# Layer 2 of a mixture-of-experts trunk: experts in fixed order, one at a time, in place of a computed order with six pairs

## What is computed

```python
g_sel = top-1 group of 4;  e_sel = top-2 of the 8 experts in that group      # per token
combine = (T, 32), two entries per token, the others zero
y = 0
for e in range(32):
    he = silu(t @ w_gate[e]) * (t @ w_up[e])          # 1024 -> 256, twice
    y = y + combine[:, e, None] * (he @ w_down[e])    # 256 -> 1024
```

## Time and profile before

| what | value |
|---|---|
| median of 3 runs | 684.5 us |
| the profiled execution's own time | 686.16 us |
| its span in the trace | 684.5 us |
| TensorE busy | 630.1 us, 92% of the span |
| VectorE, ScalarE, GpSimd busy | 36%, 18%, 9% |
| DMA queue of SyncE | 272.65 MB, 95.4% of 16 engines' span |
| mean granted TensorE clock | 0.987 of full speed |

### The profile page before, as it was taken

The page is one execution under the profiler, slowest core; times in us unless marked ns, Lnnn a source line. Parts: engine busy times, 40 slices in busy tenths (PEclk is TensorE's granted clock), DMA queues, the critical chain, the costliest instruction groups (busy, mean ns, idle before and its releaser), DMA issues.

```text
span 684.5 us, 12945 instructions
## 1 busy us (share of the span) xinstructions
PE 630.1 (92%) x4798; PEld 384.4 (56%) x4798; DVE 249.7 (36%) x664; ACT 120.8 (18%) x313; POOL 61.0 (9%) x187
## 2 busy tenths in 40 slices
PE   4899899999899999999999999999999996898995
PEld 1455465555455455556888788877644442455442
DVE  1024423222322223235679497137423230222233
ACT  4013530000000000014144234138000000000003
POOL 7000011101101101100000000001111110000100
PEclk9999999999999999999999999999999998999998
DMA  8999999999999999999997989966999999999992
GB/s 353 417 419 423 426 425 428 430 432 432 425 432 431 432 425 426 426 421 419 420 420 314 374 344 431 421 272 252 373 414 425 426 424 421 426 427 422 429 413 100
DMA packets 27690, 273.32 MB, mean 399 GB/s; under 512 B 3188, under 2 KB 3700, under 8 KB 4984
## 3 DMA queue, kind: packets, MB, share of 16 engines
q1 hardware_dynamic: 27640, 272.65, 95.4%
HBM read 271.59 MB, written 1.05 MB: 398 GB/s over the span
## 4 chain that ended last, share of the span: by engine, by line
PE 84%; DMA 9%; issue 4%; DVE 1%; ACT 1%; SPq 1%; ACTq 0%; DVEq 0%
PE bank L847 74%; DMA ring<-in_ada_w_dram 9%; PE bank L1055 7%; PE bank L1264 2%; PE bank L1582 1%; SPq L509 0%; ACT hx L2097 0%; PE bank L1436 0%; PE bank L1443 0%; DVE ye L2138 0%; ACT reg_b L1903 0%; DVE ye L2135 0%; ACTq L180 0%; DVE xh L2404 0%; DVE reg_c L2138 0%
## 5 line engine op out<-in xcount | busy, mean ns | idle before, releaser
L847 PE MATMUL bank<-ring,xh 128*64 128x256 f32 (+2 forms) x2496 | 305.7, 429 | 29.9 <-issue 29.0
L847 PEld LDWEIGHTS bank<-ring,xh 128*64 128x64 f32 (+1 forms) x2496 | 169.9, 134 | 126.8 <-issue 71.4
L2135 DVE TENSOR_TENSOR reg_c<-reg_c,bank 128x128 f32<-128x128 f32 x58 | 16.7, 288 | 175.7 <-ACT reg_c L1789 96.4
L775 POOL COPY xh<-reg_a 128x256 f32 (+1 forms) x106 | 41.7, 404 | 405.5 <-PE bank L847 281.7
L847 PE MATMUL bank<-reg_b,ring 128*128 128x256 f32 x256 | 57.2, 380 | 0.4 <-ACT reg_b L1948 0.4
L1055 PE MATMUL bank<-ye,reg_b 32*128 32x512 f32 (+1 forms) x432 | 52.8, 599 | 0.0
L847 PEld LDWEIGHTS bank<-reg_b,ring 128*128 128x128 f32 x256 | 48.0, 190 | 7.1 <-issue 0.9
L2404 DVE COPY xh<-bank 128x128 f32<-128x128 f32 x58 | 16.6, 286 | 94.9 <-PE bank L847 94.9
L2135 DVE TENSOR_TENSOR ye<-bank,reg_c 128x512 f32<-128x512 f32 (+1 forms) x60 | 40.1, 670 | 29.8 <-PE bank L847 29.8
L847 PE MATMUL bank<-ring,cact 128*32 128x512 f32 (+1 forms) x320 | 35.5, 555 | 14.4 <-DMA ring<-in_ada_w_dram 14.3
L1789 ACT ACTIVATE reg_c<-bank 128x128 f32<-128x128 f32 x32 | 8.9, 277 | 203.9 <-PE bank L847 203.9
(11 more groups left out here) (210 smaller groups left out, 458.5 us busy)
## 6 DMA issues: line engine op xcount, KB each, us to landing
ring<-in_exp_w_dram SPq DMA_DIRECT2D x38, 2048.0 KB, 19.5
ring<-in_exp_w_dram SPq DMA_DIRECT2D x20, 3072.0 KB, 16.0
ring<-in_exp_w_dram SPq DMA_DIRECT2D x50, 1024.0 KB, 18.7
ring<-in_ada_w_dram SPq DMA_DIRECT2D x48, 1024.0 KB, 17.2
ring<-in_w_qkv_dram SPq DMA_DIRECT2D x12, 1024.0 KB, 16.8
ring<-in_w_o_dram SPq DMA_DIRECT2D x4, 1024.0 KB, 8.1
gu_spare<-in_exp_w_dram SPq DMA_DIRECT2D x1, 2048.0 KB, 20.9
hx<-in_exp_w_dram SPq DMA_DIRECT2D x2, 1024.0 KB, 19.9
```

The source lines that it names most:

```text
L775: nc.gpsimd.tensor_copy(xe[:, b, k0:k1, t * CAP:(t + 1) * CAP], hS[:, k0:k1, bass.ds(off, CAP)])\
L847: return nc.tensor.matmul(o_, l_, r_, start=start, stop=stop)
L2135: return nc.vector.tensor_tensor(o_, a_, b_, op)
```

## The change

Layer 2 takes its 32 experts one at a time in fixed order 0 to 31, as layer 1 does. Gone are `order_experts`, `order_rows`, `keep_order`, `places_by_rows`, the second and third table (`table_light`, `take_light_table`) and everything of pairs. The experts outside the ring are now 4, 8 and 12. Experts 14 to 29 run in loops of 4 on all engines (GpSimd and SyncE have their own bounds), the others are written out. The last two experts have a new order on TensorE and VectorE, `last_two`. SyncE asks for the last weights in the order gate and up of 30, gate and up of 31 in halves, down of 29, 30, 31 (before: down of 29 ahead of gate and up of 31). Layer 1 is the same. The core of the diff:

```diff
-ALONE = ({R: R}, {4: R, 5: FREED, 6: SPARE})
-FRONT = R + 2
-LIGHTS = [(STAT + 2 * n, STAT + 2 * n + 1) for n in range(NLP)]
-UNITS = [(0,), (1,), (2,), (3,), (7,), (8,), LIGHTS[0], (4,), LIGHTS[1], (5,), LIGHTS[2], (6,)] + LIGHTS[3:] \
-    + [(p,) for p in range(STAT + 2 * NLP, E)]
+ALONE = ({R: R}, {4: R, 8: FREED, 12: SPARE})
+FRONT = (R + 2, 14)
+LOOPED = tuple(f + (E - f) // R * R for f in FRONT)
...
@@ SyncE @@
-            for e in (STAT - 2, STAT - 1):
-                gate_up_by_halves(e)
-            down_part(1, STAT - 2, *exp_at(1, STAT - 2))
-            sp.wait_ge(S("off_ready"), 3)
-            for p in range(STAT - 1, E):
...
+            gate_up_by_halves(5)
+            gate_up_by_halves(6)
+            down_part(1, 5, *exp_at(1, 5))
+            ring_experts = [e for e in range(6, E) if e not in ALONE[1]]
+            def following(e, i=0):
+                after = ring_experts[ring_experts.index(e) + 1]
+                s, turn = exp_at(1, after)
+                gate_up(1, after + i * R, s, turn + i)
+                s, turn = exp_at(1, e)
+                down_part(1, e + i * R, s, turn + i)
...
+            gate_up(1, e + 1, *exp_at(1, e + 1))
+            s, turn = exp_at(1, e + 2)
+            sp.wait_ge(S("ring_free", s), turn)
+            lower_part(1, e + 2, s)
+            upper_part(1, e + 2, s)
+            for e in range(LOOPED[1] - 1, E):
+                down_part(1, e, *exp_at(1, e))
...
@@ TensorE @@
                 last.then_inc(S("gu_ready", 1), 1)
-                order_rows()
                 table(1)
                 turn_he_of(1, 0, 0)
-                pe.wait_ge(S("counts_read"), 3)
                 down_of(1, 0, *loaded(1, 0), 0, clear=False)
...
+            def last_two():
+                e = E - 2
+                turn_he_of(1, e - 1, 1)
+                hidden_of(1, e, *loaded(1, e), 0)
+                turn_he_of(1, e, 0)
                 last_hidden()
-                rows_unit(u - 2, 1)
-                turn_he_of(1, u, 1)
-                down_unit(u - 1, 0, True)
+                down_of(1, e - 1, *loaded(1, e - 1), 1)
+                add_rows_of(1, e - 2, 0)
+                turn_he_of(1, e + 1, 1)
+                down_of(1, e, *loaded(1, e), 0)
+                add_rows_of(1, e - 1, 1)
...
@@ VectorE @@
                 if L:
                     nc.vector.memset(hS[:, :, NSLOT:PAD], 0.0).then_inc(S("hS_pad"), 1)
-                    order_experts()
                     take_gathered(L)
...
+            def last_two():
+                e = E - 2
+                take_heT(1, e - 1, 1)
+                match(1, e - 2)
+                dve.wait_ge(S("rows_added", 1), e - 3)
+                take_ye(1, e - 2, 0)
+                match_rows(1, e - 2, 0)
+                gate_he(1, e, 0)
+                take_heT(1, e, 0)
+                gate_he(1, e + 1, 1)
+                match(1, e - 1)
+                dve.wait_ge(S("rows_added", 1), e - 2)
+                match_rows(1, e - 1, 1)
+                take_ye(1, e - 1, 1)
+                take_heT(1, e + 1, 1)
...
```

More of the change, by code:

```diff
@@ L115, in constants @@
     rank4 = np.broadcast_to(np.arange(NG, 0, -1, dtype=np.float32) * np.float32(2.0 ** 125), (P, NG))
[L116 to L119, removed]
     misc = np.concatenate([slopes, first8, first32, rank4, quarter, one_of4, pull,
                            of_eight.astype(np.float32), in_eight.astype(np.float32),
-                           of_expert, of_expert + lane, lane - FAR, tile, part, second, light], 1)
+                           of_expert, of_expert + lane, lane - FAR, tile], 1)
     return {"misc": np.ascontiguousarray(misc)}
@@ L213, in program @@
         o += 2 * E + 2
-        own_part, second = cst[:, o:o + 1], cst[:, o + 1:o + 2]
-        light_lane = cst[:, o + 2:o + 2 + T]
-        NE = o + 2 + T
+        NE = o
         iota, alibi = cst[:, NE:NE + NSLOT], cst[:, NE + NSLOT:NM]
[L218 to L234, removed]
         ones = sb("ones", [P, P])
@@ L675, in _ @@
             down_part(1, last, SPARE, 0)
-            for e in (STAT - 2, STAT - 1):
-                gate_up_by_halves(e)
-            down_part(1, STAT - 2, *exp_at(1, STAT - 2))
-            sp.wait_ge(S("off_ready"), 3)
-            for p in range(STAT - 1, E):
[L681 to L692, removed]
+            gate_up_by_halves(5)
[8 more added lines that the diff above has]
+                down_part(1, e + i * R, s, turn + i)
+            for e in ring_experts:
+                if e < FRONT[1] - 1:
+                    following(e)
+            with sp.Fori(0, (LOOPED[1] - FRONT[1]) // R) as i:
+                for u in range(R):
+                    following(FRONT[1] - 1 + u, i)
+            e = LOOPED[1] - 1
+            gate_up(1, e + 1, *exp_at(1, e + 1))
[5 more added lines that the diff above has]
+                down_part(1, e, *exp_at(1, e))
+            sp.wait_ge(S("dn_ready", 1), early + 1)
             sp.dma_start(gfin, final_norm_g.rearrange("(a d) -> a d", a=1).broadcast_to([P, D]))\
@@ L779, in pick_tokens @@
                 copy_tokens(L, offset(L, e, t), b, t)
[L781 to L801, removed]
             def overflow(L):
@@ L826, in _ @@
                 pick_tokens(L, 1, 1, 1)
[L827 to L836, removed]
+                with pool.Fori(1, E // 2) as i:
+                    for b in range(2):
+                        pool.wait_ge(S("gu_ready", L), i * 2 + (b - 1))
+                        for t in range(T):
+                            pick_tokens(L, i * 2 + b, b, t)
+                pool.wait_ge(S("gu_ready", L), E)
                 with pool.If(beyond(pool, L) > 0):
@@ L1023, in table @@
             def table(L):
[L1025 removed]
+                pe.wait_ge(S("diag_ready"), L * T + T)
                 for g in range(4):
@@ L1191, in expert_at @@
                 down_of(L, 0, *loaded(L, 0), 0, clear=False)
[L1193 to L1210, removed]
-                                last = mm(bank[b][g:g + CAP, 0:F], xe[:, b, k, x * CAP:(x + 1) * CAP], w[x][:, k, j, :, :],
-                                          k == 0, k == KC - 1)
-                last.then_inc(S("gu_ready", 1), 1)
             def last_hidden():
@@ L1253, in rows_unit @@
-            def rows_unit(u, b):
-                if len(UNITS[u]) == 1:
-                    add_rows_of(1, u, b)
-                    return
-                pe.wait_ge(S("share_ready", 1), u + 1)
-                pe.wait_ge(S("ye_ready", 1), u + 1)
-                waited()
-                for t in range(T):
-                    for half in range(2):
-                        rows = slice(64 * half, 64 * half + 64)
-                        last = nc.tensor.matmul(bank[4 + half + 2 * t][:, :], share_light[rows, b, t, :], ye[rows, b, :],
-                                                start=False, stop=False, skip_group_check=True)
-                last.then_inc(S("rows_added", 1), 1)
@@ L1324, in later_experts @@
             def later_experts(L):
-                n = COUNTED[L]
-                if L == 0:
-                    experts(L, FRONT, LOOPED)
-                    for e in range(LOOPED, E):
-                        expert_at(L, e)
-                else:
-                    for u in range(2, NU - 1):
-                        expert_unit(u)
-                    last_unit()
+                n = E
+                experts(L, FRONT[L], LOOPED[L])
+                for e in range(LOOPED[L], E if L == 0 else E - 2):
+                    expert_at(L, e)
+                if L:
+                    last_two()
                 n_ovf = beyond(pe, L)
@@ L1427, in _ @@
             gather(0)
-            for e in range(FRONT):
+            for e in range(FRONT[0]):
                 expert_at(0, e)
@@ L1704, in _ @@
             first_hidden(1)
-            second_units()
+            second_of_halves()
+            for e in range(2, FRONT[1]):
+                expert_at(1, e)
             later_experts(1)
@@ L1852, in overflow @@
                     nc.scalar.activation(sil[:, 0, :], bank[0][:, 0:P], ACT.Silu).then_inc(S("sil_ready", L), 1)
[L1853 removed]
+                    act.wait_ge(S("rows_added", L), i + E)
             def later_experts(L):
[L1856 to L1862 removed]
+                experts(L, FRONT[L], LOOPED[L])
+                for e in range(LOOPED[L], E):
+                    expert_at(L, e)
                 n_ovf = beyond(act, L)
[L1864 removed]
+                if L:
+                    for e in (E - 2, E - 1):
+                        free_down(L, e - 1, exp_at(L, e - 1)[0])
+                free_down(L, E, exp_at(L, E - 1)[0])
                 with act.If(n_ovf > 0):
@@ L2091, in _ @@
             evac_gather(1)
+            for e in range(FRONT[1]):
+                expert_at(1, e)
             later_experts(1)
@@ L2336, in keep_order @@
-            def keep_order():
-                dve.wait_ge(S("counts"), 3)
-                nc.vector.tensor_copy(order_kept, order_at).then_inc(S("counts_read"), 1)
```

(23 more changed lines are left out.)

237 lines of the change are left out of this document (37 added, 200 removed).

## The result

The changed kernel takes 694.34 us, the median of 4 runs (694.24 to 694.58), against 684.51 for the kernel before (4 runs, 683.92 to 685.61): a ratio of 1.0143, 95% interval 1.0131 to 1.0156. The forecast was 692.5 with a range of 690.5 to 696.0, and slower. The profiled execution took 694.58 us; its span is 692.8.

The account below looks back on a forecast made before the run. The prediction took weights to bound the kernel before, TensorE the changed one. Splitting six pairs cost +29.7 us, the stall +0.95, less 16.0, 3.8, 2.1 and 0.4: +8.4; the schedule gave +8.1. With 8.0 taken: 692.5 us, range 690.5 to 696.0.

Parts of the forecast that it names:

- The bound: Layer 2 of the kernel before: weights arriving at 424 to 425 GB/s set the pace, TensorE close behind with 15.96 us of waits.
- TensorE's schedule: Layer 2 matmuls timed from the turn at 486.6 us, two experts per 12.86 us, giving +8.1 us at TensorE's end.
- the tail stall of 0.95: After gate and up of expert 30: silu and `gate_he` no longer covered by down matmuls, +0.95 us, bounds 0.5 and 2.
- the end of 684.85: TensorE's last matmul in layer 2: predicted at 684.85 us, with 7.7 us of norm and stores untouched after it.
- three requests: Weight requests for gate and up of experts 10, 14 and 17, waiting on lone experts' slots: asked at 509.0, 534.7, 560.4.
- the ledger: Layer 2's weight stream worked out request by request: pauses of 1.2 and 3.5 us, last landing 676.4, no TensorE waits expected.
- nine MiB follow each pause: Weight stream after each request held up by a lone expert: nine MiB at 2.47 us each, lasting to 535.9 and 559.3.
- rival B: Weight stream falls behind at 513 to 563 us, where its queue runs shallow: 693.9 to 698.7 us; chance 0.11.
- The margin at the last down part: End of layer 2: last weights land at 676.4, TensorE wants them at 681.1; smallest margin about 2.8 at experts 29 and 30.
- Rival C: Added TensorE work fits into its waits at 563 to 652 us, weight stream sets both ends: 684.5 or 683; chance 0.04.
- I add the difference to the median: Whole kernel: 8.0 us added to the median of 684.5, not to the profiled run's 686.16, giving 692.5 us.
- the two sums: TensorE's added time in layer 2 reckoned twice: +8.4 us from differences, +8.1 us as a schedule; 8.0 taken.

Follow-up runs that it names:

- 8, 6 and 4 pairs: Kernel before with 8 or 4 pairs of experts in place of its own 6: 684.54 us with 8, 684.68 with 4; 684.51 with 6.
- straight code: Kernel before with its computed order, unlooped code and old tail, but every expert alone and the pairs' tables gone: 694.02 us, ratio 1.013.
- 2 pairs: Kernel before with 2 pairs of experts in place of 6, the list of units written out: 686.25 us, ratio 1.002.

## Why the prediction was right, and the size by which it was off

- **The bound.** "In layer 2 the kernel before is bound by the weights" holds: 8, 6 and 4 pairs take the same time.
- **TensorE's schedule.** Of its steps, 486.6 came out as 486.51, 499.4 as 499.35, 666.6 as 666.48, the tail stall of 0.95 as 0.95, the end of 684.85 as 685.08. The 0.2 at the end come from the new order of the last matmuls, which costs 1.28 us and not 0.95, less 0.1 at the start. That `order_experts` and the loops cost nothing is borne out: no gap stands at any of them, and straight code takes 167.2 us from the turn at 499 to the turn of 29 (499.58 to 666.80), the loops 167.1.
- **The stream.** Its three requests came within 0.2 us of the ledger. The last landing was 1.6 us later than 676.4. The step that the ledger had wrong is that nine MiB follow each pause without a break. They do not come at once: in the third pause, behind the lone expert 12, only three MiB are asked for (560.36 and 560.88), and the next request is made at 567.89, when gate and up of expert 14 are done. It lands 8.9 us later, at 576.8, and that is 6.5 us after the three MiB are in (570.3), where the full stream takes 4.9 for its two MiB. These 1.6 us are the whole lateness; from 576.8 on the last 41 MiB land at 2.47 us each, as written. The first three MiB after the requests of 508.78 and 534.71 are followed late in the same way (5.3 us and 6.0), and the request of 508.78, where the ledger had no pause, lands 7.2 us after the part before it; the waits for a slot that come later hide these. That was near rival B's place, and B's direction was right, its size too large. The margin at the last down part was 3.2 us in place of 4.7, and the smallest one, at gate and up of 29 and 30, 1.1 in place of 2.8. No wait came of it, by a good deal less than was written.
- **Rival C** (the work fits into the waits) fails by the price per pair, 4.9 us where C needed less than 3.6: the waits hold two pairs less (4 pairs), and not quite four less (2 pairs), let alone six.
- **Where the size went wrong.** Measured against 684.51, the change is +9.8 us; the text said +8.0. The failing step is the last one: "I add the difference to the median". The profiled execution of before took 686.16 us. The 25 and the 17 runs of the same kernel beside two of the experiments reach 685.95 and 686.15 at most, with medians of 685.01 and 684.91: the profiled execution was an unusually long one. TensorE waits for the stream in this kernel, so it is most likely the stream that varies; no short execution of it was profiled to show this. A difference taken from the long one is too small by its excess over the median, 1.65 us: between the two profiled executions (686.16 and 694.58) the change is 8.4 us, close to the 8.1 and 8.4 of the two sums. TensorE's schedule has no such spread: the changed kernel's 4 runs lie within 0.34 us. When the bound passes to TensorE, the excess of the profiled execution drops out, and it is the absolute end that carries over: 684.85 + 7.7 = 692.55 of span, plus the 1.66 us outside the span, is 694.2 us, against 694.34 measured. The conversion accounts for 1.65 of the 1.84 us by which the forecast was low, the tail for the rest.

## What to carry to other kernels

Where two resources race, write each as a schedule with its own end and compare the ends; the price of an edit is nothing until the ends cross and full price after it (8, 6, 4 pairs: 684.5, 685.0, 684.7; 2: 686.3; none: 694.0). When the bound changes hands, as it did here, predict the absolute end of the new bound in the profiled execution, not a difference on top of a median that the old bound made. And a buffer that is loaded ahead gives time once, but while it is used no slot comes free: three such experts in a row cost 5 us here, spread out they cost nothing.

## What the runs showed of the hardware that was not expected

The weight stream stayed below its full rate in a stretch where few requests were queued, though the DMA engines show as busy (share 0.98 to 1.00). With gate and up in requests of 2 MiB it had 389 and 392 GB/s from 490 to 505 us in the two kernels (389 to 403 in all that leave this stretch as it was). With the first two of them in halves, and each first half asked for 1.8 us earlier against the requests before it, it was 423 in both. Which of the two did it, the size or the earlier request, was not taken apart. The Trainium skill, "DMA: Bandwidth & Descriptors", section Specifications, gives about 358 GB/s as the limit from HBM for a core, as half of its stack's 716, and 435 as that of the fabric. Here, where one core runs alone, whole stretches went at 423 to 425, above the first and just under the second.

Spread went with the bound in these kernels. With 10 runs each, the kernel of 2 pairs, which TensorE bounds, varied by 0.9 us, those of 4 and 8 pairs, which the stream bounds, by 3.6 and 2.5. With 4 runs each, the changed kernel varied by 0.3 us and the kernel before by 1.7.
